# Input projection of a hybrid attention layer: fp32 products replaced by three fp32r products, in two token passes

## The chip, the cores and the metric

One core of a Trainium2 chip runs the whole program. The metric is the device time of one execution in microseconds, the median of several runs; lower is better. All weights and activations are float32 in HBM.

## The reference

One layer over 1024 latent tokens `x` and 256 context tokens `ctx`, width 1024:

```python
mod   = silu(c) @ w_ada + b_ada            # (6144,), for the latents
mod_c = silu(c_ctx) @ w_ada + b_ada        # the same for the context
sh1, sc1, ga1, sh2, sc2, ga2 = split(mod, 6)
h  = rmsnorm(x, g_pre_mix) * (1 + sc1) + sh1
hc = rmsnorm(ctx, g_pre_mix) * (1 + csc1) + csh1
qa, ka, va, qb, kb, vb    = split(h  @ w_in)   # widths 512, 128, 128, 512, 512, 512
qac, kac, vac, qbc, kbc, vbc = split(hc @ w_in)
qa, ka = axial_rope(qa), axial_rope(ka)
# window attention of group A, neighbourhood attention of group B, both also over the context keys
mix = concat(rmsnorm(oa), rmsnorm(ob)) @ w_out
x = x + ga1 * rmsnorm(mix)
# then 32 experts, 4 per token, and the second residual
```

The case is about `h @ w_in` and `hc @ w_in`: 1280 tokens by 1024 by 2304 (the context needs no queries), and what surrounds it in `front`.

## The kernel before

`Kernel.build` runs `front`, `attention`, `middle`, `experts` and `combine` one after another; each is a block with one instruction stream per engine, and all engines meet between blocks. Only `front` is touched. SP (SyncE) and POOL (GpSimd) issue the DMAs, each through a queue of its own.

*Prologue of `front`.* TensorE (`ada(u)`, L573) multiplies the two condition vectors by the first four 512-column units of `w_ada`. ScalarE takes the mean square of each 128-token tile (`mean`), VectorE scales it (`scale`), TensorE transposes it (`to_columns`, L584), and both turn it into `hT` with scale and shift (`affine`, VectorE four of the eight 128-row blocks, L477, ScalarE the other four, L419). This needs `aff`, made from the four units (L497 to L501).

*Projection.* A list `groups` (L301) is worked through by all engines in step. A group is one PSUM tile. For queries and keys it is 128 weight columns by 512 tokens (256 for the context part), with the weights stationary. For values it is one 128-token tile by 256 or 128 weight columns, with `hT` stationary, so that values come out token by token, as attention wants them. Each group is a sum of eight fp32 matmuls over the 1024 inputs (L637). Four PSUM banks are used in turn; group g waits until group g-4 is copied out. The weights `w_in` come through SP in units of 512 columns (2 MB) into the two halves of `ring` (L349).

Per group ScalarE evacuates the bank (L443, L447, L455). Keys are kept as a high and a low fp32r part: ScalarE writes the high part and VectorE subtracts it from the bank (L553). For `qa` and `ka` the bank goes to `raw`, TensorE multiplies it by a permutation (`rotate`, L614), and VectorE combines both with cosines and sines (`rotated`, L527 to L539). Two tiles of `x` are transposed after each of the first three groups (L642).

*Late units.* The other eight units of `w_ada` are not multiplied on TensorE but summed on VectorE (`late_piece`, L503, an instruction per 128 rows), two pieces of 512 KB per group, loaded by SP (`load_late`, L358) into two slots. TensorE adds each sum over partitions (`sum_late`, L618).

*Skewed bias.* POOL fills a table `skew_d` in HBM with zeros (L398), writes the position bias into it in rows of 124 bytes (L401), and copies a shifted view of it, in rows of 256 bytes, to `bias_d` (L403). Each of the three waits for the one before. Nothing else is queued on POOL then.

Of the kernel before, what the change touches and what calls it, by code (L numbers as in the profile page):

```python
# [249 lines left out]
def front(K):  # L250
    nc, io, ps, ring = K.nc, K.io, K.psum, K.ring
# [3 lines left out]
    with ctx:  # L255
        sb, sem = scope(K, ctx)
        hT = sb("hT", [P, KD, SEQ + CTX])
        EARLY = 4
        LATE = 6 * D // UNIT - EARLY
        PIECE = 2  # L260
        PIECES = LATE * (KD // PIECE)
        late = sb("late", [P, 2, PIECE, UNIT])
        modrow = late[0:2, :, :, :].rearrange("p a b n -> p (a b n)")
        late_bias, late_row = late[0:LATE, 0, 0, :], late[0:LATE, 0, 1, :]
        unit_of = sb("unit_of", [P, LATE, LATE])
        cosT, sinT = sb("cosT", [P, SEQ]), sb("sinT", [P, SEQ])
        perm = sb("perm", [P, P])
        raw = sb("raw", [P, 2, UNIT])
        squares = raw[:, :, :].rearrange("p a n -> p (a n)")
        rot = K.keep[:, :].rearrange("p (a n) -> p a n", n=UNIT)  # L270
        partial = rot
        crow, csig, csilu, grow = (rot[0:16, 0, P * n:P * (n + 1)] for n in range(4))
# [4 lines left out]
        IN_V = 6  # L277
        in_v = K.v[:, :, :].rearrange("p t n -> p (t n)")[:, 0:IN_V * D].rearrange("p (t n) -> p t n", n=D)

        def xin(t):  # L280
            return in_v[:, t, :] if t < IN_V else K.qa[:, t - IN_V, :]

        const_loaded, c_loaded, b_loaded = sem("const_loaded"), sem("c_loaded"), sem("b_loaded")
        mod_stored_late = sem("mod_stored_late")
        unit_loaded = [sem("unit_loaded0"), sem("unit_loaded1")]
        unit_used = sem("unit_used")
        late_loaded = [sem("late_loaded0"), sem("late_loaded1")]
        late_used, partial_done, partial_summed, late_done = sem("late_used"), sem("partial_done"), sem("partial_summed"), sem("late_done")
        x_loaded = [sem(f"x_loaded{t}") for t in range((T + TC) // 2)]
        x_scaled, xt_done, ht_dve, ht_act = sem("x_scaled"), sem("xt_done"), sem("ht_dve"), sem("ht_act")  # L290
        ss_done, rms_done = sem("ss_done"), sem("rms_done")
        sig_done, silu_done, ct_done, ct_copied = sem("sig_done"), sem("silu_done"), sem("ct_done"), sem("ct_copied")
        ada_done, mod_done = sem("ada_done"), sem("mod_done")
        gain_loaded, modc_t, aff_done = sem("gain_loaded"), sem("modc_t"), sem("aff_done")
        group_done, group_copied, k_low = sem("group_done"), sem("group_copied"), sem("k_low")
        late_bias_loaded = sem("late_bias_loaded")
        perm_done, rope_done = sem("perm_done"), sem("rope_done")
        eps_set, skew_zeroed, skew_stored = sem("eps_set"), sem("skew_zeroed"), sem("skew_stored")
        bias_stored, dve_own, unit_of_set = sem("bias_stored"), sem("dve_own"), sem("unit_of_set")

        groups = []  # L301
        for u, tiles in ((2, [("qb", 2), ("qb", 3), ("kb", 0), ("kb", 1)]),
                         (3, [("kb", 2), ("kb", 3), ("vb", 0)]),
                         (4, [("vb", 1)]),
                         (0, [("qa", j) for j in range(4)]),
                         (1, [("ka", 0), ("va", 0), ("qb", 0), ("qb", 1)])):
            unit, col = [], 0
            for kind, j in tiles:
                width = 2 * P if kind == "vb" else P
                if kind in ("va", "vb"):  # L310
                    unit += [(u, kind, j, col, tt, width) for tt in range(T + TC)]
                else:
                    unit += [(u, kind, j, col, hf, UNIT) for hf in range(2)]
                    if kind in ("ka", "kb"):
                        unit.append((u, kind, j, col, 2, CTX))
                col += width
            groups += sorted(unit, key=lambda g: g[4]) if u == 2 else unit
        in_units = [2, 3, 4, 0, 1]
        ropes = [g for g, x in enumerate(groups) if x[1] in ("qa", "ka") and x[4] < 2]
        keys = [g for g, x in enumerate(groups) if x[1] == "kb" or x[1] == "ka" and x[4] == 2]  # L320

        def key_part(g, low):
            _, kind, j, _, hf, width = groups[g]
            cols = slice(hf * UNIT, hf * UNIT + width)
            return K.ka[:, low, cols] if kind == "ka" else K.kb[:, 2 * j + low, cols]

        ON_DVE = 4
        FIRST_PIECE = 2
        FIRST_SUM = 6
# [3 lines left out]
        @block.sync  # L333
        def _(sp):
            sp.dma_start(crow[0:8, :], io["c"][0].rearrange("(k p) -> k p", p=P)).then_inc(c_loaded, 16)
            sp.dma_start(crow[8:16, :], io["c_ctx"].rearrange("(k p) -> k p", p=P)).then_inc(c_loaded, 16)
            sp.dma_start(K.ident[:, :], io["k_ident"]).then_inc(c_loaded, 16)

            def load_x(t):
                src = io["x"][0][t * P:(t + 2) * P, :] if t < T else io["ctx"][0][(t - T) * P:(t - T + 2) * P, :]  # L340
                to = in_v[:, t:t + 2, :] if t < IN_V else K.qa[:, t - IN_V:t - IN_V + 2, :]
                sp.dma_start(to, src.rearrange("(a p) d -> p a d", p=P)).then_inc(x_loaded[t // 2], 16)

            def load_unit(n):
                if n >= 2:
                    sp.wait_ge(unit_used, n - 1)
                src, u = (w_ada, n) if n < EARLY else (w_in, in_units[n - EARLY])
                cols = min(UNIT, src.shape[2] - u * UNIT)
                sp.dma_start(ring[:, n % 2, :, 0:cols], src[:, :, u * UNIT:u * UNIT + cols]).then_inc(unit_loaded[n % 2], 16)  # L349

            def load_late(m):
                if m >= 2:
                    sp.wait_ge(late_used, m - 1)
                else:
                    sp.wait_ge(modc_t, 1)
                u, c = divmod(m, KD // PIECE)
                cols = slice((EARLY + u) * UNIT, (EARLY + u + 1) * UNIT)
                sp.dma_start(late[:, m % 2, :, :], w_ada[:, PIECE * c:PIECE * (c + 1), cols]).then_inc(late_loaded[m % 2], 16)  # L358

            load_unit(0)  # L360
            load_x(0)
            load_unit(1)
            load_x(2)
            load_unit(2)
            load_x(4)
            load_unit(3)
            for t in range(6, T + TC, 2):
                load_x(t)
            load_unit(4)
            load_unit(5)  # L370
            for m in range(PIECES):
                load_late(m)
            for n in range(6, EARLY + 5):
                load_unit(n)

            sp.wait_ge(late_used, PIECES)
            sp.dma_start(late_bias, io["b_ada"][0, EARLY * UNIT:].rearrange("(u n) -> u n", n=UNIT)).then_inc(late_bias_loaded, 16)
            sp.wait_ge(late_done, 2)
            sp.dma_start(K.mod_d[0, EARLY * UNIT:].rearrange("(u n) -> u n", n=UNIT), late_row).then_inc(mod_stored_late, 16)
            sp.wait_ge(mod_stored_late, 16)  # L380
            sp.wait_ge(bias_stored, 16)

        @block.gpsimd
        def _(pool):
            pool.memset(K.eps[:, :], EPS).then_inc(eps_set, 1)
# [5 lines left out]
            pool.memset(unit_of[:, :, :], 0.0).then_inc(unit_of_set, 1)  # L391
            pool.wait_ge(unit_of_set, 1)
            pool.memset(unit_of[:, :, :].rearrange("p a b -> p (a b)")[:, 0:LATE * LATE:LATE + 1], 1.0).then_inc(unit_of_set, 1)

            pool.wait_ge(x_loaded[(T + TC) // 2 - 1], 16)
            for dst, src in ((perm[:, :], io["k_perm"]), (cosT[:, :], io["k_cos"]), (sinT[:, :], io["k_sin"])):
                pool.dma_start(dst, src).then_inc(const_loaded, 16)
            pool.dma_start(K.skew_d.rearrange("q n k -> q (n k)"), io["k_zeros"].to_broadcast([GRID_W, BROWS * BW])).then_inc(skew_zeroed, 16)  # L398
            pool.wait_ge(skew_zeroed, 16)
            rpb = raw_ap(io["rpb_b"], 0, [[0, GRID_W], [RPB_C, NHB * RPB_R], [1, RPB_C]])  # L400
            pool.dma_start(raw_ap(K.skew_d, 2 * BW, [[BROWS * BW + 1, GRID_W], [BW, NHB * RPB_R], [1, RPB_C]]), rpb).then_inc(skew_stored, 16)  # L401
            pool.wait_ge(skew_stored, 16)
            pool.dma_start(K.bias_d, K.skew_d[:, :, NA_COLS - 1:NA_COLS - 1 + GRID_W]).then_inc(bias_stored, 16)  # L403

        @block.scalar
        def _(act):
# [1788 lines left out]
```

## Time and profile before

| | us |
|---|---|
| median of 3 runs | 2574.79 (2574.77 to 2578.52) |
| the profiled execution, time | 2576.32 |
| the profiled execution, span | 2574.4 |
| mean granted TensorE clock, share of full | 0.969 |
| TensorE busy | 2411.0 (94%) |
| VectorE busy | 1803.0 (70%) |
| ScalarE busy | 1460.7 (57%) |
| `front` ends at | 366.3 |

The span runs from the first to the last instruction. Busy time of PE is matmuls in flight; PEld is the weight loads, which overlap them. A matmul's recorded duration is its latency, so the rate is read from the distance between starts. A float32 matmul shows as two records, a fp32r matmul as one.

### The profile page before, as it was taken

How to read it: one execution, taken by the hardware profiler on the slowest of the kernel's cores; microseconds unless marked ns; L12 is line 12 of the kernel's file. 1: busy time of each engine (PE TensorE's matmuls, PEld its weight loads, DVE VectorE, ACT ScalarE, POOL GpSimd, SP SyncE). 2: the span in 40 equal slices, each digit the busy share in tenths (PEclk: the TensorE clock that was granted, in tenths of full speed). 3: DMA queues.
4: the chain of work that ended last, by engine and by line, in shares of the span. 5: the costliest groups of instructions: out<-in, count | busy, mean ns of one | idle time of the engine just before them, and what ended most of it. 6: DMA issues, size and time to landing. Idle time of an engine off the chain costs nothing. (4 is left out here: it accounts for less than half of the span.)

```text
span 2574.4 us, 37126 instructions
## 1 busy us (share of the span) xinstructions
PE 2411.0 (94%) x12354; PEld 1842.9 (72%) x12354; DVE 1803.0 (70%) x2383; ACT 1460.7 (57%) x1827; POOL 389.7 (15%) x297
## 2 busy tenths in 40 slices
PE   7999989999688399999999999999999999999987
PEld 2567467887577287878777777788888888888862
DVE  2440316766564688888888888877777777877866
ACT  3201027777532477777767677666656666666752
POOL 1000013233022101010101020211210210210310
PEclk8999999999898699999999999999999999999998
DMA  9751026434332499999999998978968978978988
GB/s 355 151 162 66 0 69 164 99 91 117 118 131 92 182 332 318 352 329 338 341 330 342 321 350 307 363 249 295 328 244 293 332 248 293 326 253 290 342 299 326
DMA packets 296053, 639.52 MB, mean 248 GB/s; under 512 B 12146, under 2 KB 13394, under 8 KB 295810
## 3 DMA queue, kind: packets, MB, share of 16 engines
q1 hardware_dynamic: 277970, 571.29, 64.3%
q0 software_dynamic: 18000, 67.13, 7.3%
q8 instruction: 52, 0.85, 0.1%
q14 instruction: 31, 0.25, 0.0%
HBM read 599.69 MB, written 44.65 MB: 250 GB/s over the span
## 5 line engine op out<-in xcount | busy, mean ns | idle before, releaser
L1799 DVE TENSOR_TENSOR w_lo_x<-wring,w_hi_x 128x2048 fp32r<-128x2048 f32 x444 | 1008.5, 2285 | 53.1 <-ACT w_hi_x L1640 25.2
L1640 ACT ACTIVATE w_hi_x<-wring 128x2048 fp32r<-128x2048 f32 x444 | 843.0, 1911 | 51.0 <-DMA wring<-in_w_mlp 49.7
L2011 PE MATMUL psum<-w_hi_x,x_hi_x 128*128 128x512 f32 x992 | 417.2, 421 | 10.3 <-DVE w_lo_x L1799 10.3
L2013 PE MATMUL psum<-w_hi_x,x_lo_x 128*128 128x512 f32 x992 | 388.8, 392 | 0.0
L2012 PE MATMUL psum<-w_lo_x,x_hi_x 128*128 128x512 f32 x992 | 388.1, 391 | 0.0
L2008 PE MATMUL psum<-w_hi_x,x_both_x 128*128 128x512 f32 x640 | 270.8, 423 | 0.0
L1603 POOL TENSOR_TENSOR poolgate_x<-poolgate_x 128x1 f32<-128x1 f32 x61 | 64.0, 1049 | 1261.5 <-DVE y_x L1844 830.5
L2009 PE MATMUL psum<-w_lo_x,x_both_x 128*128 128x512 f32 x640 | 250.7, 392 | 0.0
L2011 PEld LDWEIGHTS psum<-w_hi_x,x_hi_x 128*128 128x128 f32 x992 | 188.8, 190 | 45.9 <-DVE w_lo_x L1799 12.6
L2013 PEld LDWEIGHTS psum<-w_hi_x,x_lo_x 128*128 128x128 f32 x992 | 186.9, 188 | 41.6
L2012 PEld LDWEIGHTS psum<-w_lo_x,x_hi_x 128*128 128x128 f32 x992 | 187.8, 189 | 36.4
L637 PE MATMUL psum<-hT,ring 128*128 128x512 f32 (+1 forms) x496 | 202.4, 565 | 3.3 <-DVE hT L481 2.5
L2011 PE MATMUL psum<-w_hi_x,a_hi_x 128*128 128x512 f32 x496 | 196.6, 396 | 1.8 <-DVE y_x L1844 1.8
L2013 PE MATMUL psum<-w_hi_x,a_lo_x 128*128 128x512 f32 x496 | 193.6, 390 | 0.0
L2012 PE MATMUL psum<-w_lo_x,a_hi_x 128*128 128x512 f32 x496 | 193.3, 390 | 0.0
L637 PEld LDWEIGHTS psum<-hT,ring 128*128 128x128 f32 x496 | 94.2, 192 | 108.2 <-issue 106.3
L2009 PEld LDWEIGHTS psum<-w_lo_x,x_both_x 128*128 128x128 f32 x640 | 120.6, 189 | 23.3
L2008 PEld LDWEIGHTS psum<-w_hi_x,x_both_x 128*128 128x128 f32 x640 | 120.9, 189 | 21.8
L2008 PE MATMUL psum<-w_hi_x,a_both_x 128*128 128x512 f32 x320 | 125.9, 393 | 0.0
L853 ACT ACTIVATE S<-S,least 128x640 f32<-128x640 f32 (+3 forms) x128 | 114.0, 890 | 19.0 <-DVE least L924 11.4
L2009 PE MATMUL psum<-w_lo_x,a_both_x 128*128 128x512 f32 x320 | 124.6, 389 | 0.0
L768 POOL TENSOR_TENSOR bias<-bias,keep 128x2560 f32<-128x2560 f32 x16 | 90.7, 5666 | 183.5 <-DMA keep<-in_k_mask_b 164.1
(326 smaller groups left out, 3641.1 us busy)
## 6 DMA issues: line engine op xcount, KB each, us to landing
wring<-in_w_mlp SPq DMA_DIRECT2D x444, 1024.0 KB, 6.1
bias<-bias_d SPq DMA_DIRECT2D x32, 640.0 KB, 7.8
late<-in_w_ada SPq DMA_DIRECT2D x32, 512.0 KB, 3.8
yg<-y_d SPq DMA_DIRECT2D x32, 512.0 KB, 7.1
ring<-in_w_ada SPq DMA_DIRECT2D x4, 2048.0 KB, 8.5
ring<-in_w_in SPq DMA_DIRECT2D x4, 2048.0 KB, 10.0
ring<-in_w_out SPq DMA_DIRECT2D x2, 2048.0 KB
mix_d<-o SPq DMA_DIRECT2D x16, 256.0 KB, 4.0
```

Source lines behind the costliest of these rows:

```text
L637: last = pe.matmul(ps[:, g % 4, 0:width], lhs, rhs, start=(k == 0), stop=(k == KD - 1))
L768: pool.tensor_tensor(rows, rows, mask_b.rearrange("p (a n) -> p a n", a=1).to_broadcast([P, HEADS, LB]), ALU.add).then_inc(bias_ready, 1)
L853: act.activation(row, row, ACT.Exp, bias=least[:, s:s + 1], scale=-1.0, accum_out=den[:, s:s + 1]).then_inc(p_done, 1)
L1603: pool.tensor_tensor(poolgate[:, 1:2], poolgate[:, 0:1], poolgate[:, 0:1], ALU.add).then_inc(gate_open, 1)
L1640: act.activation(w_hi[:, u % HI, k, :], ring[:, u % RING, k, :], ACT.Copy).then_inc(hi_done, 1)
L1799: dve.tensor_tensor(w_lo[:, u % LO, k, :], ring[:, u % RING, k, :], w_hi[:, u % HI, k, :].bitcast(F32), ALU.subtract).then_inc(lo_done, 1)
L2008: pe.matmul(bank, both[:, k, r - 1, :], w_hi[:, u % HI, k, :], start=(not biased and k == 0), stop=False)
L2009: last = pe.matmul(bank, both[:, k, r - 1, :], w_lo[:, u % LO, k, :], start=False, stop=(k == KD - 1))
L2011: pe.matmul(bank, hi[:, k, :], w_hi[:, u % HI, k, :], start=(not biased and k == 0), stop=False)
L2012: pe.matmul(bank, hi[:, k, :], w_lo[:, u % LO, k, :], start=False, stop=False)
L2013: last = pe.matmul(bank, lo[:, k, :], w_hi[:, u % HI, k, :], start=False, stop=(k == KD - 1))
```

## The change

- The projection is computed as three fp32r products instead of one fp32 product: `w_hi*h_hi + w_hi*h_lo + w_lo*h_hi`, where `hi` is the value rounded to fp32r and `lo` the remainder.
- The tokens go in two passes of five tiles each: context and latent tiles 0 to 2, then latent tiles 3 to 7. In each pass a 128-column unit of weights is multiplied by 256 and by 384 tokens (queries skip the context, so they have only the 384 in the first pass). There are 28 groups in the first pass and 36 in the second (`BORDER` = 28). Each weight unit is loaded twice, 512 KB a load, three raw buffers deep.
- ScalarE rounds each weight unit (`weights_high`) and VectorE takes the remainder (`weights_low`), in both passes. The same is done to each tile of h (`rounded`, `remainder`).
- Weights are now always stationary, so values come out transposed. They go through a buffer `stage` and are turned back by TensorE transposes (`turn`), and VectorE copies them to `v` (`finish`). `qa` and `ka` use the same `stage`.
- The tiles of the second pass are transposed in the last eight groups of the first pass and at the border.
- The late units are now loaded by POOL, in 64 pieces of 256 KB (one instruction of VectorE each) into two slots, and the three steps of the skewed bias stand between them in POOL's queue.
- `w_ada` units go to the space of `qaT` and `qbT`; the raw weights, rows and staging lie in `ring`.

The core of the diff:

```diff
+        units = kb[0:2] + staged + qb + kb[2:4] + kb[0:2] + staged + kb[2:4] + qb
+        # staged = va, vb0..3, ka, qa0..3; units[0:18] are the first pass
+        last_of = [max(g for g, x in enumerate(groups) if x[0] == u) for u in range(2 * PER)]
+        prepared = {last_of[u - 2] + 1: u for u in range(2, 2 * PER)}
+        COLS = (slice(0, TC * P), slice(TC * P, PASS * P))
+        pieces = [0] * FIRST_PIECE + [1] * (BORDER - FIRST_PIECE)
+        pieces += [2 if n < rest - (len(groups) - BORDER - 4) else 1 for n in range(len(groups) - BORDER - 4)] + [0] * 4
+        MEANS, TURNS_AT = 6, BORDER - 8
...
@@ SP
-            for m in range(PIECES):
-                load_late(m)
+            for u in range(RAW, 2 * PER):
+                load_w(u)              # waits for w_low of unit u - 3
...
@@ POOL
+            load_late(0)
+            load_late(1)
+            pool.dma_start(K.skew_d..., zeros).then_inc(skew_stored, 16)
+            for m in range(2, 16):
+                load_late(m)           # waits for late_used >= m - 1
+            pool.wait_ge(skew_stored, 16)
+            pool.dma_start(K.skew_d..., rpb).then_inc(skew_stored, 16)
+            for m in range(16, 32):
+                load_late(m)
+            pool.wait_ge(skew_stored, 32)
+            pool.dma_start(K.bias_d, K.skew_d...).then_inc(skew_stored, 16)
+            for m in range(32, PIECES):
+                load_late(m)
...
@@ ACT
+            for i in range(PASS):
+                affine(i)
+                rounded(i)
+                if i == 1:
+                    weights_high(1)
+            for g in range(len(groups)):
+                if g == BORDER:
+                    rounded(PASS + 2)
+                    for i in range(PASS + 3, 2 * PASS):
+                        affine(i)
+                        rounded(i)
+                evacuate(g)
+                if g + 1 in prepared:
+                    weights_high(prepared[g + 1])
...
@@ DVE
+            for g in range(len(groups)):
+                if g == BORDER:
+                    remainder(PASS + 2)
+                    for i in range(PASS + 3, 2 * PASS):
+                        affine(i)
+                        remainder(i)
+                if g in keys:
+                    ...
+                if g + 1 in prepared:
+                    weights_low(prepared[g + 1])
+                if g - 1 in stages:
+                    finish(stages.index(g - 1))
+                for m in range(first_piece[g], first_piece[g + 1]):
+                    late_piece(m)
...
@@ PE
+            def to_columns(i, half):
+                pe.wait_ge(x_scaled, i + 1)
...
+                else:
+                    bank = 7 if half else 4 + i % 2
+                    pe.wait_ge(stage_done, EARLY_STAGES)
...
+            def project(g):
+                u, kind, j, part = groups[g]
+                pe.wait_ge(w_low, u + 1)
+                pe.wait_ge(h_low, (PASS if u >= PER else 0) + (PASS if part else TC))
...
+                for k in range(KD):
+                    pe.matmul(bank, w_hi[:, u % 2, k, :], hT_hi[:, k, rows], start=(k == 0), stop=False)
+                    pe.matmul(bank, w_hi[:, u % 2, k, :], hT_lo[:, k, rows], start=False, stop=False)
+                    last = pe.matmul(bank, w_lo[:, u % 2, k, :], hT_hi[:, k, rows], start=False, stop=(k == KD - 1))
...
+            for g in range(len(groups)):
+                project(g)
+                if g - 1 in stages:
+                    turn(stages.index(g - 1))
+                if g in sums:
+                    sum_late(sums[g])
+                if TURNS_AT <= g < TURNS_AT + 4:
+                    to_columns(PASS + (g - TURNS_AT) // 2, (g - TURNS_AT) % 2)
+                if g == BORDER - 2: both halves of to_columns(PASS + 2)
+                if g == BORDER - 1: to_columns(PASS + 3, 0)
+                if g == BORDER: to_columns(PASS + 3, 1), both halves of to_columns(PASS + 4)
```

## Rows read from the trace of the kernel before

**Rows 1.** Busy time of each engine by stage: window, its length, engines, clock, DMA share, GB/s
```profile
core 0: us, PE busy (x) PEld busy (x) DVE busy (x) ACT busy (x) POOL busy (x), PEclk, DMA share, GB/s
...
45.90:54.80 8.90, 3.88 (x16) 3.15 (x17) 8.50 (x24) 5.91 (x16) 0.00 (x0) 0.51 1.09 422
54.80:366.30 311.50, 309.40 (x1060) 182.43 (x1060) 90.04 (x144) 36.20 (x85) 5.17 (x2) 0.99 0.34 88
...
54.00:59.50 5.50, 4.68 (x6) 2.13 (x7) 0.56 (x2) 0.00 (x0) 0.37 (x1) 0.50 0.81 254
```

**Rows 2.** Groups of instructions of 54.8 to 366.3 us: count, busy, mean ns, idle before
```profile
L637 PE MATMUL psum<-hT,ring 128*128 128x512 f32 x416 | 184.4, 600 | 3.3 <-DVE hT L481 2.5 <-PE psum L637 0.8
...
L637 PE MATMUL psum<-ring,hT 128*128 128x256 f32 x320 | 70.3, 380 | 0.4 <-PE psum L637 0.4
L515 DVE SCALAR_TENSOR_TENSOR keep<-late,cT,keep 128x512 f32<-128x512 f32 x56 | 42.1, 751 | 22.0 <-DMA late<-in_w_ada 20.6
...
L423 ACT ACTIVATE hT<-psum,aff 128x128 f32<-128x128 f32 x24 | 8.7, 469 | 21.8 <-PE psum L590 21.8
...
L529 DVE TENSOR_TENSOR keep<-psum,sinT 128x512 f32<-128x512 f32 x10 | 6.9, 692 | 46.6 <-PE psum L614 46.6
...
L553 DVE TENSOR_TENSOR kbT<-psum,kbT 128x256 fp32r<-128x256 f32 x4 | 1.7, 425 | 1.3 <-ACT kbT L447 1.0 <-DVE keep L515 0.2
```

**Rows 3.** Timeline, weight loads: start us, length us, fp32 with 512, transposes, 256, 128 columns
```profile
60.32 0.19 PEld L637 LDWEIGHTS psum<-hT,ring 128*128 128x128 f32 x1 [0.24 <-issue]
60.75 0.19 PEld L637 LDWEIGHTS psum<-hT,ring 128*128 128x128 f32 x1 [0.24 <-issue]
...
64.18 1.67 PEld L590 LDWEIGHTS psum<-ident,v 128*128 128x128 f32 x15 [0.29 <-issue]
...
204.90 4.08 PEld L637 LDWEIGHTS psum<-ring,hT 128*128 128x128 f32 x19
...
325.83 3.32 PEld L637 LDWEIGHTS psum<-ring,hT 128*128 128x128 f32 x29
```

**Rows 4.** Timeline, weight loads of the experts' fp32r products with 512 columns
```profile
1203.06 0.19 PEld L2013 LDWEIGHTS psum<-w_hi_x,x_lo_x 128*128 128x128 f32 x1
...
1203.51 0.19 PEld L2012 LDWEIGHTS psum<-w_lo_x,x_hi_x 128*128 128x128 f32 x1
1203.74 0.19 PEld L2013 LDWEIGHTS psum<-w_hi_x,x_lo_x 128*128 128x128 f32 x1
```

**Rows 5.** Timeline, weight loads of attention's fp32r products, 256 columns, two half-arrays in turn
```profile
382.24 0.31 PEld L797 LDWEIGHTS psum<-kaT,qh 64*128 64x128 f32 x4
382.48 0.19 PEld L797 LDWEIGHTS psum<-kaT,ql 64*128 64x128 f32 x2
```

**Rows 6.** The page's costliest groups: how weights are split in the experts
```profile
L1799 DVE TENSOR_TENSOR w_lo_x<-wring,w_hi_x 128x2048 fp32r<-128x2048 f32 x444 | 1008.5, 2285 | 53.1 <-ACT w_hi_x L1640 25.2
L1640 ACT ACTIVATE w_hi_x<-wring 128x2048 fp32r<-128x2048 f32 x444 | 843.0, 1911 | 51.0 <-DMA wring<-in_w_mlp 49.7
```

**Rows 7.** Groups of instructions of 375 to 640 us: copies out of PSUM of 384 columns
```profile
L953 DVE COPY PT<-psum 128x384 f32<-128x384 f32 x32 | 17.8, 555 | 9.3 <-PE psum L808 8.7
...
L868 ACT ACTIVATE PT<-psum 128x384 f32<-128x384 f32 x12 | 5.9, 490 | 6.3 <-PE psum L808 6.3
```

**Rows 8.** Timeline of the first tiles of h and the first product
```profile
45.93 2.90 ACT L423 ACTIVATE hT<-psum,aff 128x128 f32<-128x128 f32 x8 [1.97 <-DVE aff L501]
...
51.06 1.36 DVE L481 TENSOR_SCALAR hT<-psum,aff 128x128 f32<-128x128 f32 x4
...
54.82 9.53 PE L637 MATMUL psum<-hT,ring 128*128 128x512 f32 x16 [2.49 <-DVE hT L481]
```

**Rows 9.** DMAs issued in 41 to 70 us: KB each, median us to landing
```profile
late<-in_w_ada SPq DMA_DIRECT2D x2, 512.0 KB, 29.1
skew_d<-in_rpb_b POOLq DMA_DIRECT2D x1, 930.0 KB, 29.5
```

**Rows 10.** DMA queues in 70 to 84 us: packets, MB, share of 16 engines
```profile
q0 software_dynamic: 151, 0.52, 88.3%
q1 hardware_dynamic: 6, 0.01, 2.5%
```

**Rows 11.** DMAs issued in 90 to 104 us, beside the second copy
```profile
late<-in_w_ada SPq DMA_DIRECT2D x3, 512.0 KB, 8.4
...
bias_d<-skew_d POOLq DMA_DIRECT2D x1, 1984.0 KB, 14.8
```

**Rows 12.** DMAs issued in 660 to 700 us, several at once on POOL's queue
```profile
ring<-in_b_mlp POOLq DMA_DIRECT2D x3, 256.0 KB, 4.2
gate<-mod_d POOLq DMA_DIRECT2D x1, 512.0 KB, 7.7
...
gain<-in_g_pre_ffn POOLq DMA_DIRECT2D x1, 512.0 KB, 12.5
...
b_router<-in_b_router POOLq DMA_DIRECT2D x1, 16.0 KB, 12.3
```

More of the change, by code:

```diff
@@ L301, in front @@
-        groups = []
[L302 to L317, printed above, removed]
@@ L318, in front @@
-        in_units = [2, 3, 4, 0, 1]
-        ropes = [g for g, x in enumerate(groups) if x[1] in ("qa", "ka") and x[4] < 2]
-        keys = [g for g, x in enumerate(groups) if x[1] == "kb" or x[1] == "ka" and x[4] == 2]
-        def key_part(g, low):
[L323 to L329, printed above, removed]
+        turned, stage_done = sem("turned"), sem("stage_done")
@@ new lines, in front @@
+        PER = len(names)
+        groups = []
+        for u, (kind, j) in enumerate(units):
+            if u < PER:
+                groups += [(u, kind, j, part) for part in ((1,) if kind[0] == "q" else (0, 1))]
+            else:
+                groups += [(u, kind, j, part) for part in range(2)]
+        BORDER = sum(g[0] < PER for g in groups)
+        groups[BORDER + 1], groups[BORDER + 2] = groups[BORDER + 2], groups[BORDER + 1]
+        last_of = [max(g for g, x in enumerate(groups) if x[0] == u) for u in range(2 * PER)]
@@ new lines, in front, with is_context, out_cols, width_of @@
+        prepared = {last_of[u - 2] + 1: u for u in range(2, 2 * PER)}
+        COLS = (slice(0, TC * P), slice(TC * P, PASS * P))
+        def is_context(g):
+            return groups[g][0] < PER and groups[g][3] == 0
+        def out_cols(g):
+            if is_context(g):
+                return slice(SEQ, SEQ + CTX)
+            start = COLS[groups[g][3]].start + (FIRST_LATER * P if groups[g][0] >= PER else -TC * P)
+            return slice(start, start + width_of(g))
+        def width_of(g):
+            return COLS[groups[g][3]].stop - COLS[groups[g][3]].start
@@ new lines, in turn_cols @@
+        def turn_cols(g):
+            start = COLS[groups[g][3]].start - (TC * P if groups[g][0] < PER else 0)
+            return slice(start, start + width_of(g))
+        turns = [g for g, x in enumerate(groups) if x[1] in ("qa", "ka") and not is_context(g)]
+        stages = [g for g, x in enumerate(groups) if x[1] in ("va", "vb") or g in turns]
+        keys = [g for g, x in enumerate(groups) if x[1] == "kb" or x[1] == "ka" and is_context(g)]
+        EARLY_STAGES = sum(g < BORDER for g in stages)
@@ new lines, in front @@
+        FIRST_PIECE = 2
+        pieces = [0] * FIRST_PIECE + [1] * (BORDER - FIRST_PIECE)
+        rest = PIECES - sum(pieces)
+        pieces += [2 if n < rest - (len(groups) - BORDER - 4) else 1 for n in range(len(groups) - BORDER - 4)] + [0] * 4
+        assert sum(pieces) == PIECES
+        first_piece = [sum(pieces[:g]) for g in range(len(groups) + 1)]
+        sums = {min(g for g in range(len(groups)) if first_piece[g + 1] >= (u + 1) * KD) + 1: u for u in range(LATE)}
+        MEANS, TURNS_AT = 6, BORDER - 8
@@ L331, in front @@
+        def key_part(g, low):
+            _, kind, j, _ = groups[g]
+            return K.ka[:, low, out_cols(g)] if kind == "ka" else K.kb[:, 2 * j + low, out_cols(g)]
         block = ctx.enter_context(nc.Block())
@@ L351, in load_late @@
[L351 to L363, printed above, removed]
@@ L419, in affine @@
-            def affine(t):
-                r = 0 if t < T else 1
-                act.wait_ge(xt_done, t + 1)
-                for k in range(ON_DVE, KD):
-                    last = act.activation(hT[:, k, t * P:(t + 1) * P], ps[:, 4 + 2 * (t % 2) + k // 4, (k % 4) * P:(k % 4 + 1) * P],
-                                          ACT.Identity, bias=aff[:, r, 1, k:k + 1], scale=aff[:, r, 0, k:k + 1])
-                last.then_inc(ht_act, 1)
-            for t in range(T + TC):
-                mean(t)
@@ new lines, in affine @@
+            def affine(i):
+                r = 1 if i < TC else 0
+                act.wait_ge(xt_done, 2 * i + 2)
+                if i >= 2:
+                    act.wait_ge(h_low, i - 1)
+                bank = 5 + 2 * (i % 2) if i < PASS else 7
+                for k in range(4, KD):
+                    last = act.activation(rows_in[:, i % 2, k, :], ps[:, bank, (k - 4) * P:(k - 3) * P], ACT.Identity, bias=aff[:, r, 1, k:k + 1], scale=aff[:, r, 0, k:k + 1])
+                last.then_inc(ht_act, 1)
@@ new lines, in affine @@
+            def affine(i):
+                r = 1 if i < TC else 0
+                dve.wait_ge(xt_done, 2 * i + 1)
+                if i >= 2:
+                    dve.wait_ge(h_high, i - 1)
+                    dve.wait_ge(h_low, i - 1)
+                bank = 4 + 2 * (i % 2) if i < PASS else 4 + i % 2
+                for k in range(4):
+                    last = dve.tensor_scalar(rows_in[:, i % 2, k, :], ps[:, bank, k * P:(k + 1) * P], aff[:, r, 0, k:k + 1], aff[:, r, 1, k:k + 1], ALU.mult, ALU.add)
+                last.then_inc(ht_dve, 1)
@@ new lines, in _ @@
+                if g in range(MEANS + 1, MEANS + 1 + PASS):
+                    scale(g - MEANS - 1 + PASS)
+                if g == TURNS_AT + 1:
+                    affine(PASS)
+                if g == TURNS_AT + 3:
+                    affine(PASS + 1)
+                if g == BORDER - 2:
+                    remainder(PASS)
+                    remainder(PASS + 1)
+                    affine(PASS + 2)
+            dve.wait_ge(late_stored, 16)
+            dve.wait_ge(partial_summed, LATE)
@@ L594, in _ @@
             ada(1)
-            to_columns(0)
+            for half in range(2):
+                to_columns(0, half)
             ada(2)
-            to_columns(1)
+            for half in range(2):
+                to_columns(1, half)
             ada(3)
@@ L603, in _ @@
                 last = pe.transpose(ps[:, 2, 2 * n:2 * n + 2], modrow[0:2, n * P:(n + 1) * P], K.ident[0:2, 0:2])
[L604 to L614 removed]
+            last.then_inc(columns_done, 1)
@@ new lines, in _ @@
+            for i in range(2, PASS):
+                for half in range(2):
+                    to_columns(i, half)
+            def project(g):
+                u, kind, j, part = groups[g]
+                pe.wait_ge(w_low, u + 1)
+                pe.wait_ge(h_low, (PASS if u >= PER else 0) + (PASS if part else TC))
+                if g < 4:
+                    pe.wait_ge(aff_done, 4)
+                else:
+                    pe.wait_ge(group_copied, g - 3)
+                    pe.wait_ge(k_low, sum(k <= g - 4 for k in keys))
+                bank, rows = ps[:, g % 4, 0:width_of(g)], COLS[part]
+                for k in range(KD):
+                    pe.matmul(bank, w_hi[:, u % 2, k, :], hT_hi[:, k, rows], start=(k == 0), stop=False)
+                    pe.matmul(bank, w_hi[:, u % 2, k, :], hT_lo[:, k, rows], start=False, stop=False)
+                    last = pe.matmul(bank, w_lo[:, u % 2, k, :], hT_hi[:, k, rows], start=False, stop=(k == KD - 1))
+                last.then_inc(group_done, 1)
@@ new lines, in turn @@
+            def turn(m):
+                g = stages[m]
+                width = width_of(g)
+                pe.wait_ge(group_copied, g + 1)
+                if m >= 2:
+                    pe.wait_ge(stage_done, m - 1)
+                if g in turns:
+                    if g == turns[0]:
+                        pe.wait_ge(const_loaded, 48)
+                    pe.matmul(ps[:, 4 + m % 2, 0:width], perm[:, :], stage[:, m % 2, 0:width], start=True, stop=True).then_inc(turned, 1)
+                    return
+                for n in range(width // P):
+                    last = pe.transpose(ps[:, 4 + m % 2, n * P:(n + 1) * P], stage[:, m % 2, n * P:(n + 1) * P], K.ident[:, :])
+                last.then_inc(turned, 1)
```

470 lines of the change are left out of this document (245 added, 225 removed).

## The prediction

> **What bounds the kernel now.** I read the busy times by stage first. `front` lasts until 366.3 us, and in its projection, 54.8 to 366.3, TensorE is busy 309.4 of 311.5 us at a granted clock of 0.99, while VectorE has 90 and ScalarE 36 us of work [rows 1]. So this stretch is TensorE's, and what shortens TensorE's work there shortens the kernel, as long as nothing else takes over. In the groups of instructions TensorE waits almost nowhere; VectorE's only waits on its own account are 20.6 us for the late pieces, which hide [rows 2]. The later blocks start when `front` ends and are not touched, so the whole effect is the shift of 366.3. The profiled execution took 2576.3 us and the median is 2574.8; I take the shift from the span and apply it to the median.
>
> **The products.** The columns that stream through TensorE are the same before and after: 8 query units by 1024 tokens and 10 others by 1280, 20,992 columns for each of eight input blocks. fp32 costs 0.43 us for each of two records at 512 columns, 4.08/19 = 0.215 at 256 and 3.32/29 = 0.114 at 128 [rows 3]: four cycles a column at 2.4 GHz and nearly nothing beside. That is 20,992 x 8 x 4 / 2400 = 279.9 us. Beside it stand ten permutations of 512 columns (8.5), eight sums of late units (6.8) and 48 transposes at 0.11 (1.67 us for 15, [rows 3]; 5.3), together 300.5. Of the 311.5 measured, 2.7 more are the half clock at the start (0.50 over 5.5 us, [rows 1]); the rest, 8 us, is switching between instructions of different kinds and short waits. I keep 7.5 of it for the new stream.
>
> fp32r in the experts starts a 512-column product every 0.68/3 = 0.227 us [rows 4]: 0.213 of streaming and 0.013 on top. At 256 columns attention shows 0.24 us for two pairs [rows 5], 0.120 a pair, again 0.013 above the stream. I take 0.120 for 256 and 0.173 for 384 columns. There are 28 groups of 256 and 36 of 384, 24 products each: 672 x 0.120 + 864 x 0.173 = 80.6 + 149.5 = 230.1 us. The bounds are 210 (nothing on top) and, if a load of 128 columns (0.053 at 2.4 GHz) came out whole between products, 230 + 1536 x 0.040 = 291.
>
> Of this price the Trainium skill has a rule that speaks against the change: "TensorE: Matmul & The Clock Gate", Part 3, says that a weight load overlaps matmuls in flight only when it goes to another row group. By that rule the sum would go to the upper bound, 61 us more; the full-height loads of the experts [rows 4] contradict it at 512 columns, where only 0.013 shows, and nothing in the trace shows full-height fp32r at 256.
>
> **What is added on TensorE.** 50 transposes of values, 5.5 us at 0.11; permutations and sums stay (8.5 + 6.8); 40 transposes of x come into the stream, 4.4, for 48 before. New stream: 230.1 + 5.5 + 8.5 + 6.8 + 4.4 + 7.5 = 262.8 us.
>
> **The start.** The prologue up to `aff` at 45.9 has the same transfers and products. Then each tile of h is a chain. VectorE's half of the affine takes 1.36 us, ScalarE's four take 1.45 [rows 8]. The rounding over 1024 columns takes half of 1911 ns, the remainder half of 2285 [rows 6]. Only then comes VectorE's next affine: about 3.75 with handoffs. Five tiles and one weight unit in between (1.2) end at 45.9 + 18.7 + 1.2 = 65.8. The first group (context, two tiles) runs before that, behind the last transposes at about 58, at half clock; the second needs all five tiles. So from 65.7 on 262.8 - 2.9 = 259.9 us are left, which gives 325.6 without any stall. The late start costs 11 us against 54.8 and is contained in this.
>
> **VectorE and ScalarE under it.** 34 weight units at 1.15 are 39 us for VectorE. The 64 pieces are 48 as before; finishing takes 38 (the rotations are as before, value copies at 0.555 for 384 columns [rows 7] are new), keys 8, the second pass's tiles 17: 150 of 260. ScalarE: 34 roundings at 0.96, 64 copies at about 0.45 (0.49 at 384 columns [rows 7]), the tiles: 84. Neither bounds on the whole. The tightest stretch is qa in the first pass, one group per weight unit: TensorE 4.15 + 0.64 + 0.15 = 4.9 a group; VectorE remainder 1.15, finish 2.45 (four operations of 0.56 at 384 columns, between 692 ns at 512 and 425 at 256 [rows 2], and handoffs), piece 0.8, together 4.4. It fits with half a microsecond.
>
> **Stalls that the order brings.** (a) The first transpose of the second pass (group 20) waits for the last `finish` of the first pass, which VectorE reaches only after the weight unit of that same group: copy 0.5, rounding 1.0, remainder 1.15, finish 2.45, less the turn: 4.6 us. (b) At the border tiles 7 to 9 are a chain of 3.7 each on both engines. Tile 9 is done 12.1 us after group 27, while TensorE has 28, 29 and the transposes, 7.5: 4.6 us. (c) Three such pauses each can drop the clock to 1.2 GHz for a while, as at the start: I take 3 us.
>
> **The skewed bias now stands among the late loads.** In the trace, the write in 124-byte rows takes 29.5 us to land [rows 9], and between 70 and 84 us its queue holds 88.3% of the 16 engines and SP's 2.5% [rows 10]. An SP load of 512 KB of that time had a median of 29.1 us to landing [rows 9]. In the new kernel the write is issued when piece 13 is used, in group 15. Piece 16 is loaded behind it on the same queue. Transfers issued together on that queue landed one after another: 7.7 to 12.5 us, and 12.3 for 16 KB [rows 12]. Group 18 wants piece 16 about 20 us after group 15, and it lands at 33. VectorE then still has two remainders, two finishes and a piece before TensorE may pass the wait of (a): it resumes at 42 instead of 29.5. Weight units from SP, three buffers ahead, are slowed by the same transfer to about the same moment. I take 12 us; without these waits it is 0, and if also unit 12 is caught, 17. The first write, the zeros, ends before piece 2. The last copy, 14.8 us [rows 11], is issued in group 30, where two pieces a group are due. Piece 32 is late by 11 us; the `stage` buffers and banks let TensorE run on for four groups, so 4 us remain (0 to 8).
>
> The skill's page "DMA: Bandwidth & Descriptors", "Two DMAs through the same engine are not ordered", says that descriptors of one queue start in order on each DMA engine. By it piece 16 waits for the whole write; the landings of [rows 12] agree.
>
> **The sum.** 325.6 + 4.6 + 4.6 + 3 + 12 + 4 = 353.8 against 366.3: 12.5 us less. 2574.8 - 12.5 = 2562.
>
> The tail is not at risk: pieces end four groups (14 us) before the end, and the late row's sum, its load and its store take about 6. The bias table is complete long before attention asks for it.
>
> **Rivals.**
> - *The skew disturbs nothing* (loads slip in beside it): 16 us less, 2546. For: VectorE waited only 20.6 us for late loads in all of the old stream [rows 2]. Against: the 2.5% of [rows 10].
> - *The stalls eat it all*: both skew waits at their upper ends (17 + 8) and the border tiles a few us slower: 2571 to 2579. Same buffers, same place; it needs every chain at its worst.
> - *The late loads become the bound.* Two slots on POOL's queue carry 64 pieces, so two pieces take one round trip plus 0.85. From the first, near 74 us, this ends at 74 + 32 x (L + 0.85) + 14.6. It decides from L = 7.8 us, where it gives 366.3. At L = 8.4, what SP's loads took beside the copy [rows 11], the end is 385 and the time 2593: slower. Against: three 256 KB loads on this queue landed in 4.2 [rows 12].
> - *The weight load shows at narrow products*: the upper bound above, 61 us more: 2623, slower. For: the narrow full-height product is not in the trace. Against: 0.114 us between starts with 128-column fp32 loads [rows 3], so a load fits under a short stream.
>
> **How the numbers follow.** The forecast gets 0.50, its own range 2552 to 2574 (stalls 8 less to 12 more, handoffs). The undisturbed skew gets 0.20, the eaten gain 0.12, the late loads 0.10, the shown weight load 0.06, and 0.02 is for none of them. A measurement of this kernel tells about 0.2%, 5 us, from nothing. Faster: 0.45 of the forecast's 0.50 and the 0.20, with a little of the rest, 0.66; same: 0.05 + 0.10, 0.15; slower 0.19. The range goes from 2543, below the undisturbed case, to 2590. It leaves out the shown weight load, half of the late loads and a little below.
>
> **What would show it.** TensorE's weight-load starts 0.120 and 0.173 us apart in the projection; the second group starting near 66 us; `front` ending near 354; a pause of TensorE of 15 us or more around group 20, with VectorE waiting for a `late` load and ScalarE for a raw weight unit while the 124-byte rows are written; 4 to 5 us at the border. The prediction is wrong if those starts lie 0.16 us apart, if VectorE waits for `late` all along the two passes, or if the pause around group 20 has another releaser.

## The result, and the profile after

The changed kernel takes 2586.85 us (median of 15 runs) against 2580.23 us of the kernel before (15 runs beside it): ratio 1.0024, 95% interval 1.0014 to 1.0035. The forecast was 2562, faster. The profiled execution spans 2584.8 us.

Windows of the changed kernel: the start and the projection from its second group to its last product.

```profile
core 0: us, PE busy (x) PEld busy (x) DVE busy (x) ACT busy (x) POOL busy (x), PEclk, DMA share, GB/s
45.90:66.58 20.68, 10.48 (x55) 9.51 (x54) 14.39 (x32) 13.59 (x27) 0.00 (x0) 0.64 0.63 231
66.58:369.60 303.02, 265.65 (x1648) 252.15 (x1648) 149.45 (x234) 78.46 (x136) 40.03 (x64) 0.94 0.49 125
```

Before, TensorE was busy 309.4 of 311.5 us at a clock of 0.99 [rows 1]. Now 37 of 303 us are idle, and the clock is 0.94. Attention's first product starts at 372.1 us instead of 368.1.

Timeline of weight loads, changed kernel, with 256 columns and then with 384:

```profile
103.28 0.19 PEld L745 LDWEIGHTS psum<-hT_lo,w_in_hi 128*128 128x128 f32 x1
103.40 0.19 PEld L746 LDWEIGHTS psum<-hT_hi,w_in_lo 128*128 128x128 f32 x1
103.51 0.19 PEld L744 LDWEIGHTS psum<-hT_hi,w_in_hi 128*128 128x128 f32 x1
...
243.18 0.19 PEld L745 LDWEIGHTS psum<-hT_lo,w_in_hi 128*128 128x128 f32 x1
243.35 0.19 PEld L746 LDWEIGHTS psum<-hT_hi,w_in_lo 128*128 128x128 f32 x1
243.53 0.19 PEld L744 LDWEIGHTS psum<-hT_hi,w_in_hi 128*128 128x128 f32 x1
```

The starts are 0.12 and 0.17 to 0.18 us apart, as priced. So the products do what they should, and the loss is in the idle time. TensorE's waits from 54 us to attention:

```profile
PE psum L712 <- issue: 19.3, 1, 19.3
PE psum L768 <- DVEq L602: 8.9, 8, 1.8
PE psum L744 <- issue: 6.4, 2, 3.3
PE psum L761 <- ACT ring L514: 4.8, 1, 4.8
PE psum L712 <- DVE ring L577: 2.8, 1, 2.8
PE psum L712 <- ACT ring L488: 1.2, 1, 1.2
```

L712 is `to_columns`, L744 a group's first product, L768 `sum_late`, L761 the turning of values. The two waits at L744 are 3.3 us before the second group (66.58 us) and 3.1 us before group 30, behind the border (218.67 us). "issue" names nobody; what the 19.3 us were waiting for has to be read on the other engines. VectorE in that time:

```profile
144.72 0.55 DVE L619 TENSOR_TENSOR ring<-ring,cosT 128x384 f32<-128x384 f32 x1
145.31 0.56 DVE L620 TENSOR_TENSOR ring<-psum,sinT 128x384 f32<-128x384 f32 x1
145.90 1.12 DVE L625 TENSOR_TENSOR qaT<-ring 64x384 f32<-64x384 f32 x2
161.62 0.49 DVE L597 TENSOR_SCALAR keep<-ring,cT 128x512 f32<-128x512 f32 x1 [14.60 <-issue]
165.24 1.23 DVE L588 TENSOR_TENSOR w_in_lo<-ring,w_in_hi 128x1024 fp32r<-128x1024 f32 x1 [3.13 <-ACT w_in_hi L504]
166.38 0.55 DVE L619 TENSOR_TENSOR ring<-ring,cosT 128x384 f32<-128x384 f32 x1
```

It stands 14.6 us in front of late piece 16 (L597), queued behind the bias write; then 3.1 us for a weight unit that ScalarE could not round earlier, because SP's load of it was late too. TensorE has nothing from 153.8 to 173.05. The transfers issued in 134 to 139 us:

```profile
skew_d<-in_rpb_b POOLq DMA_DIRECT2D x1, 930.0 KB, 29.7
ring<-in_w_in SPq DMA_DIRECT2D x1, 512.0 KB, 29.7
ring<-in_w_ada POOLq DMA_DIRECT2D x1, 256.0 KB, 23.5
```

The DMA queues in 144 to 149 us: packets, MB, share of 16 engines (q0 carries the write, q1 SP's loads):

```profile
q0 software_dynamic: 43, 0.18, 89.8%
q1 hardware_dynamic: 45, 0.02, 17.1%
```

Over the whole kernel the same loads land in 3.9 us (512 KB, SP) and 3.3 us (256 KB, POOL). Windows of the changed kernel around three of the pauses:

```profile
66.58:73.30 6.72, 6.72 (x24) 6.72 (x25) 0.23 (x1) 0.00 (x0) 0.00 (x0) 0.57 0.73 199
173.05:179.20 6.15, 6.15 (x24) 6.15 (x25) 0.68 (x1) 0.00 (x0) 0.54 (x1) 0.58 0.32 90
250.50:255.60 5.10, 4.81 (x23) 4.81 (x24) 2.40 (x4) 1.67 (x3) 1.08 (x2) 0.50 0.80 240
```

Each holds one group of 24 products. The granted clock is mostly at its lower level (1.2 GHz), and the group, from its first start to its last, takes 6.71 us instead of 4.1, 6.09 instead of 4.0 and 5.05 instead of 2.8; a fourth, group 30, 5.62 instead of 4.1. Together 8.4 us.

### The profile page after: what moved, and what is told of

It is laid out like the page before. It is cut to its first block and busy times, and to the rows that moved or that the text cites. A ratio compares the mean times of both kernels' runs of the same rounds, so it can differ in the third digit from the quotient of the medians.

```text
span 2584.8 us, 38718 instructions
## 1 busy us (share of the span) xinstructions
PE 2379.3 (92%) x12974; PEld 1921.8 (74%) x12974; DVE 1868.6 (72%) x2474; ACT 1505.7 (58%) x1876; POOL 423.2 (16%) x361
## 5 line engine op out<-in xcount | busy, mean ns | idle before, releaser
L744 PE MATMUL psum<-hT_hi,w_in_hi 128*128 128x384 f32 (+1 forms) x512 | 170.1, 332 | 6.4 <-issue 6.4
L746 PE MATMUL psum<-hT_hi,w_in_lo 128*128 128x384 f32 (+1 forms) x512 | 163.9, 320 | 0.0
L745 PE MATMUL psum<-hT_lo,w_in_hi 128*128 128x384 f32 (+1 forms) x512 | 163.8, 320 | 0.0
```

Of the source, the lines that this page charges most:

```text
L744: pe.matmul(bank, w_hi[:, u % 2, k, :], hT_hi[:, k, rows], start=(k == 0), stop=False)
L745: pe.matmul(bank, w_hi[:, u % 2, k, :], hT_lo[:, k, rows], start=False, stop=False)
L746: last = pe.matmul(bank, w_lo[:, u % 2, k, :], hT_hi[:, k, rows], start=False, stop=(k == KD - 1))
```

## The experiments

All but the ninth start from the changed kernel. "Front" is the start of attention's first product, 372.1 us there; ratios are against the kernel before.

**1. No bias write.** The 124-byte rows are not written, so group B's scores lack the position bias; tokens then go to other experts, and only the front can be compared.

```diff
-            pool.dma_start(raw_ap(K.skew_d, ...), rpb).then_inc(skew_stored, 16)
```

> The changed kernel without the write of the position bias in 124-byte rows (left out: the bias table stays zero, so the output lacks the position bias); everything else of POOL's queue stays. Theory A (this write holds the queue and the DMA engines, and the 19.3 us pause of TensorE after group 20 comes from it, except for the 4.6 us that the order of VectorE's work costs by itself): the pause falls to 4 to 6 us, the half-clock stretch after it goes, and front ends 15 to 18 us earlier than in the changed kernel (369.9 us), near 353; time about 0.995 to 0.997 of the kernel before. Rival (the pause is the order of VectorE's and TensorE's work, the write only runs beside it): the pause stays above 12 us and front ends within 5 us of 369.9.

Front 358.1. TensorE's wait at `to_columns`, which is L710 here:

```profile
PE psum L710 <- issue: 4.5, 1, 4.5
```

The pause goes from 19.3 to 4.5 us: the write costs 14.8 us there, and 4.5 is the order's own share. The front gains 14.1 us, a little less than the 15 to 18 expected. The stretch at the lower clock had been expected to go and did not: behind the pause of 4.5 us the granted clock is 0.51 (158.2 to 164.3 us), and the waits at the sums are 10.5 us instead of 8.9.

**2. Write in eight parts**, one for each head, before pieces 6, 8, ... 20.

> The same write cut into eight, one head each, issued before pieces 6, 8, ... 20 instead of at once before piece 16. Theory A with a held queue: eight holds of about 3.7 us, each shorter than the two groups that a piece has to land, so the pause after group 20 falls to 4 to 6 us as without the write, and front ends near 353 to 357. If the engines' total occupation is what costs (the transfers have to be paid wherever they are), front ends where it did, within 5 us of 369.9, with the waits spread over groups 8 to 22.

Front 358.6, ratio 0.9977 (0.9965 to 0.9990).

```profile
PE psum L716 <- issue: 4.5, 1, 4.5
```

`to_columns` waits 4.5 us, as without any write: the bytes are harmless, the unbroken block is not.

**3. Late pieces back on SP's queue**, between the weight units; POOL only issues the skew steps.

> The late pieces are issued by SP, in the order in which VectorE frees their slots among the weight units; POOL keeps the three steps of the skewed bias, at the same points. If the pause after group 20 comes only from piece 16 standing behind the write in POOL's queue, it falls to 4 to 6 us and front ends near 354. If the write holds the DMA engines for SP's queue as well (in the changed kernel ScalarE waited 15.2 us for a weight unit that landed at 164.1 us, after the piece), the pause stays at 15 to 25 us, and front ends within 6 us of 369.9.

Front 366.6, ratio 1.0006 (0.9993 to 1.0018). TensorE's waits:

```profile
PE psum L719 <- issue: 17.6, 1, 17.6
PE psum L775 <- DVEq L609: 10.2, 7, 4.0
```

Transfers issued in 125 to 160 us:

```profile
ring<-in_w_in SPq DMA_DIRECT2D x4, 512.0 KB, 16.2
skew_d<-in_rpb_b POOLq DMA_DIRECT2D x1, 930.0 KB, 30.4
ring<-in_w_ada SPq DMA_DIRECT2D x3, 256.0 KB, 21.4
```

The pause stays, as the second expectation had it: being on another queue than the write hardly helps. The wait of 4.8 us at the copy (L761 in the changed kernel) is gone, but at the same place (250.4 us) a sum now waits 4.0 us, where the sum after the copy waited 1.4 before. So only a part of that stall was order within POOL's queue.

**4. Each sum of a late unit one group later.**

```diff
-        sums = {min(...) + 1: u for u in range(LATE)}
+        sums = {min(...) + 2: u for u in range(LATE)}
```

> TensorE's eight sums of late units stand one group later. Theory B (TensorE waits at each sum for the last piece of the unit, which VectorE makes in the same group: 8.9 us in all): all waits for the sums go, and front ends 7 to 10 us earlier, near 361; time about 0.999 to 1.000 of the kernel before. Rival (the waits move to the weights that VectorE prepares after the piece, since VectorE is what is late): front ends within 3 us of 369.9.

Front 362.7, ratio 0.9987 (0.9972 to 1.0001), 9.4 us earlier, as expected. TensorE's waits:

```profile
PE psum L712 <- issue: 20.4, 1, 20.4
PE psum L761 <- ACT ring L514: 6.1, 1, 6.1
PE psum L744 <- issue: 5.9, 2, 3.4
```

All eight waits at L768 are gone. The pause and the wait at the copy grew by 2.4 us together.

**5. Second pass's transposes one group later** (`TURNS_AT = BORDER - 7`).

> Only the transposes of the second pass start one group later (groups 21 to 24 instead of 20 to 23). Theory: of the 19.3 us pause, 4.5 us are the wait for the last finish of the first pass in the same group (4.47 us were left in the run without the bias write). In the changed kernel VectorE is held up until 161.6 us by piece 16, so TensorE now does one more group before it stops; the pause moves to group 21 or 22 and shrinks by one group's 4.2 us, and front ends near 365.5. If the pause has nothing to do with where these transposes stand, front ends within 1 us of 369.9.

Front 363.1, ratio 0.9995 (0.9983 to 1.0007): 9.0 us earlier, about twice the 4.4 expected. The pause moves from the transpose to group 21's weights and shrinks:

```profile
PE psum L744 <- DVE w_in_lo L588: 13.4, 1, 13.4
```

Once the transposes no longer wait for the last `finish`, only the late weight unit is left of it. That is 5.9 us; 1.6 us more come from a shorter wait at the copy (3.2 us), 1.0 from the sums.

**6. Write in eight parts and earlier, shifted copy in four.**

```diff
+            heads = {4 + 2 * h: h for h in range(NHB)}      # before piece m: write of head h
+            copies = {20 + 2 * n: n for n in range(4)}      # before piece m: quarter n of the copy
```

> The bias write in eight parts before pieces 4 to 18, and the shifted copy in four parts before pieces 20, 22, 24 and 26 instead of at once before piece 32. Theory: as in the run with only the write split, the pause after group 20 is 4.5 us; in addition the wait near group 35 (5.4 us there, 4.8 in the changed kernel) and its half-clock stretch (2 us) go, so that attention starts near 351 us (358.6 with the write split alone). Rival: near the border two pieces a group are due with a round trip of more than 3 us each, and this, not the copy, makes VectorE late: attention starts within 2 us of 358.6.

Front 347.8, ratio 0.9934 (0.9916 to 0.9953). The pause is 4.5 and the wait at the copy is gone: 24.3 us, of which 19.6 are these two waits. That is 3 us more than expected.

**7. Edits 4, 5 and 6 together, and groups 1 and 2 exchanged.**

```diff
+        groups[1], groups[2] = groups[2], groups[1]
```

> All of it together: write in eight parts, copy in four, sums of late units a group later, transposes of the second pass a group later, and groups 1 and 2 exchanged, so that the first two context groups run before the fifth tile is ready. If the stalls add up as worked out (372.1 less 13.5 for the write, 7.5 for the copy, 9.4 for the sums, 4.5 for the transposes, 3 for the exchange), attention starts near 334 us, 34 us before the kernel before (368.1), time 0.987 of it. If something else takes over when they go (VectorE's queue or the round trip of the pieces), it starts at 345 us or later, time 0.991 or more.

Front 327.1, ratio 0.9848 (0.9828 to 0.9868), median 2544.47 us; 334 had been expected. TensorE's waits in its front:

```profile
PE psum L749 <- issue: 3.0, 2, 2.5
PE psum L717 <- DVE ring L582: 2.8, 1, 2.8
...
PE psum L717 <- ACT ring L493: 1.2, 1, 1.2
PE psum L717 <- issue: 0.3, 1, 0.3
```

**8. One product instead of three** (the two with a low part left out), on top of 7: how low can the front go when TensorE does not bound it?

> The kernel with all fixes, with the first of the three products alone (w_lo and h_lo are still made, but the products with them are left out, so q, k and v have the precision of one fp32r product). Theory: TensorE's stream bounds the projection once the stalls are gone; 1024 products of 0.120 or 0.173 us less are 153 us less work, and front shortens until VectorE's queue (some 165 us of work, handoffs and waits for pieces at two per round trip of 3.3 us) bounds it: attention starts at 240 to 270 us. Rival (VectorE's and ScalarE's chain already bounds it): attention starts within 30 us of the kernel with all fixes.

Front 281.0, one run. The window of 46 to 250 us:

```profile
46.00:250.00 204.00, 130.57 (x590) 105.62 (x590) 146.70 (x238) 81.86 (x148) 42.33 (x66) 0.80 0.69 192
```

ScalarE's waits in it:

```profile
ACT ring L519 <- DVE v L617: 36.6, 17, 4.6
ACT ring L519 <- DVE qaT L630: 24.7, 8, 3.6
```

The front is 46 us below version 7: not down to the 240 to 270 of the theory, and further than the 30 us of the rival. ScalarE's copies to `stage` wait for VectorE's `finish`, and no engine is busy for the whole window, so this order of work seems bound by its hand-overs there.

**9. The kernel before, with its late pieces on POOL's queue.** fp32 products, groups and units are untouched; only `load_late` moves, with the write before piece 8 and the copy before piece 16.

```diff
-            for m in range(PIECES): load_late(m)      # SP
+            load_late(0); load_late(1); (zeros)       # POOL
+            for m in range(2, 8): load_late(m)
+            (write)
+            for m in range(8, 16): load_late(m)
+            (copy)
+            for m in range(16, PIECES): load_late(m)
```

> The kernel before, fp32 products and all, with one part of the change alone: its 32 late pieces (512 KB) go through POOL's queue with the three skew steps between them. Theory (a load queued behind the bias write stops the engines that need it, whatever the products cost): VectorE waits 15 to 25 us for the piece behind the write, key groups behind it on VectorE are late, and TensorE pauses 5 to 15 us; attention starts at 373 to 383 instead of 368.1, ratio 1.002 to 1.006. Rival (the pause needs the change's own order of groups and its small weight units): attention starts at 367 to 370, ratio within 0.1% of 1.

Front 394.2 against 368.1, ratio 1.0107 (1.009 to 1.0123). Timeline of VectorE at piece 8:

```profile
109.68 0.69 DVE L559 TENSOR_TENSOR kbT<-psum,kbT 128x512 fp32r<-128x512 f32 x1 [2.79 <-ACT kbT L453]
133.16 0.49 DVE L519 TENSOR_SCALAR keep<-late,cT 128x512 f32<-128x512 f32 x1 [22.79 <-DMA late<-in_w_ada]
```

Waits of TensorE and VectorE in the front:

```profile
PE psum L624 <- DVEq L527: 21.0, 5, 10.5
...
DVE keep L521 <- DMA late<-in_w_ada: 29.0, 22, 2.1
```

The wait of VectorE for the piece behind the write was as expected (15 to 25 us). TensorE's loss was not: 26.1 us, where 5 to 15 were expected, and it stands at five sums (L624, 21.0 us) and not at the key groups. The granted clock falls to 0.53 to 0.56 behind the three longest of these waits. The sums come at fixed groups, while the pieces run late by the 22.8 us and, after that, by up to 2.1 us at nearly each: this queue lands a 512 KB piece in 4.2 us.

**10. The changed kernel once more.**

> The changed kernel once more, nothing edited, beside the kernel before. Theory (all of the loss is in the front): attention starts at 372 and the ratio is 1.001 to 1.002, so 4 of the 6.6 us are the front and the rest is scatter of the untouched stages. Rival (the untouched stages are slower behind the changed front too): ratio 1.0024 again or more, with attention, middle and experts together 2 us or more longer than before.

2591.33 us, ratio 1.0025 (1.0012 to 1.0037), front 373.8 (5.7 later than before). The pause is again 19.3, the sums 10.9. The rival's conditions hold: from attention to the end of the experts the profiled execution took 2150.4 us, where the kernel before took 2141.3 and the first profile of the changed kernel 2146.6. Most of the difference is attention: 295.8 us, against 288.0 in the kernel before, 289.7 in the first profile, and 289.2 to 295.6 in experiments 2 to 7 and 9. The front explains 4.1 of the 6.6 us between the medians in the first result, and 5.7 of 8.0 here.

## Why the prediction was wrong

The last product was forecast to end at 353.8 and ended at 369.9. Term by term, in us:

| step of the prediction | forecast | measured |
|---|---|---|
| pitch at 256 and 384 columns | 0.120, 0.173 | 0.120, 0.1735 |
| second group starts | 65.7 | 66.6 |
| stream after it, at full clock | 259.9 | 257.6 (by difference) |
| (a) and the bias write, group 20 | 4.6 + 12 | 19.3 |
| (b) border | 4.6 | 1.2 + 3.1 |
| shifted copy, near group 36 | 4 | 4.8 |
| (c) clock after the start | 3 | 8.4 |
| waits at the eight sums | 0 | 8.9 |

**Right.** The price of the products, against the rule of the Trainium skill on weight loads ("TensorE: Matmul & The Clock Gate", Part 3); the start; both order stalls; the place, cause and duration of the bias write (29.5 foreseen, 29.7 measured), with VectorE at a late piece and ScalarE at a weight unit. Experiments 1, 2 and 6 confirm the write, and experiment 1 leaves the 4.5 us of (a). None of the four rivals came about as described. The eaten gain is nearest (2571 to 2579; the ratio gives 2581), but it named 17 + 8 us for the two skew waits, and they took 14.8 and 4.8.

**The failed step is "eight sums of late units (6.8)".** It priced the sums as work alone and carried them over, with the waits left to the 7.5 us of switching. But `sum_late` stands one group after the unit's last piece, and since the change that group lasts 3 to 4 us of TensorE's time, while VectorE has a weight remainder, a `finish` and one or two pieces to do in it. So TensorE catches up with VectorE at each sum, for 1.1 us on average, as here, where the unit's last piece (L599) stands behind a `finish` (L625):

```profile
140.90 1.12 DVE L625 TENSOR_TENSOR qaT<-ring 64x384 f32<-64x384 f32 x2
142.05 0.75 DVE L599 SCALAR_TENSOR_TENSOR keep<-ring,cT,keep 128x512 f32<-128x512 f32 x1
142.91 1.02 PE L768 MATMUL psum<-keep,unit_of 128*8 128x512 f32 x2 [1.16 <-DVEq L602]
```

I had worked out that VectorE fits "with half a microsecond" over a group, and that was a statement on throughput; a wait in TensorE's own order needs it at one instant. Experiment 4 shows the cause: with one group of distance all eight waits are gone, and the front is 9.4 us shorter.

**The second is a size: (c), 3 us for the clock.** Four stretches of about a group each ran mostly at the lower level, 1.5 to 2.6 us apiece. The pauses before them were 3.3, 19.3, 3.1 and 4.8 us, so the short ones cost at least about half as much again, and the longest no more than they did. It is read from windows; no experiment changes the clock alone. Windows of 2 us, TensorE's busy time times what the clock lacks in each, add up to 9.8 us in the changed kernel, 5.2 in experiment 6 and 1.5 in 7, and the fronts agree: experiment 6 gains 24.3 us, 19.6 in its two waits and 4.6 here; experiment 7 gains 45.0, of which 19.6 (bias steps), 8.9 (sums), 4.2 (transposes), 3.4 (the waits at a group's first product, 2.8 of them by the exchange) and 8.3 (clock) make 44.4.

**The third, +2.7 us,** is the pause itself: 19.3 for 16.6.

Together, with the copy, the start, the border and the stream, 8.9 + 5.4 + 2.7 + 0.8 + 0.9 - 0.3 - 2.3 = 16.1 us, which turns a gain of 12.5 into a loss of 3.6. The fronts differ by 4.1: the 366.3 that the forecast started from is where the last copy of the kernel before ended, and its last product ended at 365.7.

What is left of the 6.6 us of the medians, 2.5 us, lies behind the front, in code that the change does not touch. I had expected nothing there ("the whole effect is the shift of 366.3"), and its cause is open. Scatter alone is not shown: the median less the front is 1.1 to 3.8 us longer than in the kernel before in all eight versions with the new products (the first result, its repeat, experiments 2 to 7), and 0.2 us shorter in experiment 9, which keeps the old ones. Each front comes from one profiled execution, so this is a hint and no more. In the repeat, TensorE pauses in attention for 3.6 us and runs at 0.66 of the clock for some ten microseconds; what decides whether it does is open too.

Was it the products or the order? The order. With the same products, experiment 7 puts the front 41 us below the kernel before. And experiment 9 shows that moving the late loads among the skew steps costs 26 us even under the fp32 stream. Before, the write ran beside late loads on SP's own queue, and what VectorE lost [rows 2] did not reach TensorE.

## What to carry to other kernels

When a bound engine is made faster, go through every place where its order waits for another engine and ask how long the other has between its last input and that instant; busy shares over a stretch do not answer this. A long transfer in small rows is best cut into pieces between the urgent loads: here the cut saved 14.8 of the 19.3 us of pause (experiment 2), and moving the loads to another queue 1.7 (experiment 3). Price each pause of a few microseconds on TensorE with the stretch at the lower clock behind it.

## What the runs showed of the hardware

- **Two queues share the DMA engines by packets, not by time.** In 144 to 149 us, the write's queue moved 43 packets and SP's 45, yet they held 89.8% and 17.1% of 16 engines: 80 us x 0.898 / 43 = 1.67 us a packet of the write, 0.30 us one of SP's. The five microseconds before and after show 43 and 52, 46 and 41 packets. An estimate from these numbers: 0.93 MB in packets of 0.18 MB / 43 are about 14 for each of 16 engines, and 14 x (1.67 + 0.30) is 28 us, in which a 512 KB load moves about as many of its 64 packets of 512 bytes for each engine. So it lands only when the write is over: 29.7 us in the changed kernel, and a median of 21.4 us for the late pieces on SP's queue in experiment 3. The 151 and 6 packets of [rows 10] are not equal: there SP's queue had only the last packets of one load left, and they came singly, 1.2 to 2.0 us apart from 69.75 to 77.45 us, which is about the time of one packet of the write. The Trainium skill, "DMA: Bandwidth & Descriptors", "Queues, rings and completion order", says that each DMA engine takes turns between queues at packet granularity; the equal counts agree with it. I had not used it.
- **A full-height 128x128 weight load hides under 256 columns of fp32r**: 0.120 us from start to start, 0.107 of them columns at 2.4 GHz. The Trainium skill, "TensorE: Matmul & The Clock Gate", Part 3, says that it overlaps only with another row group; here the measurement decides against it.
